# Seven block products instead of eight in more FFN input chunks of a four-layer trunk, and the modulation sums moved to make room

## The reference

```python
def adaln(c, w, b):
    m = (jax.nn.silu(c) @ w + b).reshape(c.shape[0], N_MOD, 1, D_MODEL)
    return [m[:, i] for i in range(N_MOD)]

def swiglu(h, w_in, w_out):
    g, u = jnp.split(h @ w_in, 2, axis=-1)
    return (jax.nn.silu(g) * u) @ w_out
...
for i in range(DEPTH):
    ...
    xp = xp + mod_p[2] * mp
    xs = xs + mod_s[2] * ms
    hp = modulate(rms_norm(xp, norm2_w[i]), mod_p[3], mod_p[4])
    hs = modulate(rms_norm(xs, norm2_w[i]), mod_s[3], mod_s[4])
    xp = xp + mod_p[5] * swiglu(hp, ffn_in_w[i], ffn_out_w[i])
    xs = xs + mod_s[5] * swiglu(hs, ffn_in_w[i], ffn_out_w[i])
```

## Time and profile before

| | us |
|---|---|
| median of 3 runs | 2639.33 |
| lowest and highest | 2639.11, 2639.5 |
| the profiled execution | 2641.69 |
| its span | 2639.7 |
| TensorE busy | 2622.5 |
| VectorE busy | 1814.8 |
| ScalarE busy | 886.7 |
| GpSimd busy | 213.4 |

### The profile page before, as it was taken

One profiled execution on the slowest core, in us unless ns is written; L12 is line 12 of the kernel. 1 busy time (PEld: TensorE's weight loads), 2 busy tenths in 40 slices (PEclk: granted clock), 3 DMA queues, 4 the chain that ended last, 5 costly groups with the idle time before them and its releaser, 6 DMA issues.

```text
span 2639.7 us, 44971 instructions
## 1 busy us (share of the span) xinstructions
PE 2622.5 (99%) x17398; PEld 2551.5 (97%) x17398; DVE 1814.8 (69%) x3097; ACT 886.7 (34%) x1330; POOL 213.4 (8%) x297
## 2 busy tenths in 40 slices
PE   9999999999999999999999999999999999999998
PEld 5999999999999999999967999999999999999998
DVE  5888778676586776846676668768465557748475
ACT  4223331222342222124675432221242234425253
POOL 0000000000000000000000000000000015113020
PEclk9999999999999999999999999999999999999999
DMA  8444445444224454422101245444222224547362
GB/s 308 146 143 138 133 128 176 128 158 143 77 77 128 150 161 124 155 72 74 57 13 73 80 128 160 151 127 152 70 82 72 72 76 112 164 125 187 110 166 76
DMA packets 100025, 321.41 MB, mean 122 GB/s; under 512 B 11712, under 2 KB 14912, under 8 KB 99648
## 3 DMA queue, kind: packets, MB, share of 16 engines
q1 hardware_dynamic: 65776, 211.23, 24.6%
q0 software_dynamic: 34128, 108.54, 14.7%
HBM read 301.12 MB, written 2.88 MB: 115 GB/s over the span
## 4 chain that ended last, share of the span: by engine, by line
PE 94%; DVE 3%; DMA 1%; ACT 1%; issue 1%; DVEq 0%; POOL 0%; SPq 0%; ACTq 0%; POOLq 0%
PE ps L720 40%; PE ps L719 40%; PE ps L772 7%; PE ps_x L1018 1%; PE ps_sum L772 1%; PE ps L994 1%; PE ps L1150 1%; PE ps_sum L1005 1%; DMA mix<-in_ada_head 1%; DVE w_lo L1717 1%; PE ps L1101 0%; PE ps L875 0%; ACT w_hi L1218 0%; PE ps_sum L980 0%; DMA rope<-raw 0%
## 5 line engine op out<-in xcount | busy, mean ns | idle before, releaser
L1717 DVE TENSOR_TENSOR w_lo<-raw,w_hi 128x1024 fp32r<-128x1024 f32 (+2 forms) x319 | 383.1, 1201 | 464.3 <-ACT w_hi L1218 463.1
L1218 ACT ACTIVATE w_hi<-raw 128x1024 fp32r<-128x1024 f32 (+2 forms) x319 | 329.3, 1032 | 917.8 <-PE ps L720 902.8
L719 PE MATMUL ps<-h_hi,w_hi 128*128 128x320 f32 x1568 | 490.6, 313 | 1.3 <-DVE h_lo L2035 0.7
L720 PE MATMUL ps<-h_lo,w_hi 128*128 128x322 f32 x1568 | 489.1, 312 | 0.0
L720 PE MATMUL ps<-h_hi,w_lo 128*128 128x322 f32 x1568 | 488.0, 311 | 0.0
L719 PE MATMUL ps<-h_lo,w_hi 128*128 128x320 f32 x1568 | 487.8, 311 | 0.0
L719 PE MATMUL ps<-h_hi,w_lo 128*128 128x320 f32 x1568 | 487.5, 311 | 0.0
L720 PE MATMUL ps<-h_hi,w_hi 128*128 128x322 f32 x1568 | 486.5, 310 | 0.0
L1745 DVE CUSTOM_DVE_ANT_0 ps_x<-ada_w,cond 128x1024 f32<-128x1024 f32 x354 | 436.0, 1232 | 33.5 <-DVE tmp L1793 13.0
L720 PEld LDWEIGHTS ps<-h_hi,w_hi 128*128 128x128 f32 x1568 | 297.8, 190 | 0.6
L719 PEld LDWEIGHTS ps<-h_hi,w_hi 128*128 128x128 f32 x1568 | 296.0, 189 | 2.4 <-DVE h_lo L2035 0.8
(11 more groups left out here) (239 smaller groups left out, 4014.6 us busy)
## 6 DMA issues: line engine op xcount, KB each, us to landing
raw<-in_weights SPq DMA_DIRECT2D x323, 512.0 KB, 3.6
ada_w<-in_ada_w POOLq DMA_DIRECT2D x177, 512.0 KB, 3.8
raw<-in_weights SPq DMA_DIRECT2D x32, 384.0 KB, 3.0
rope<-in_weights SPq DMA_DIRECT2D x40, 256.0 KB, 3.2
rope<-raw POOLq DMA_DIRECT2D x40, 256.0 KB, 4.1
mix<-in_ada_head SPq DMA_DIRECT2D x16, 512.0 KB, 10.5
raw<-raw POOLq DMA_DIRECT2D x20, 256.0 KB, 3.3
x<-in_x SPq DMA_DIRECT2D x8, 320.0 KB, 10.2
```

Source lines behind the costliest of these rows:

```text
L719: pe.matmul(ps[:, 2 * slot, 0:TA], w[:, slot, ws], a(k)[:, 0:TA], start=begin, stop=end)
L720: mm = pe.matmul(ps[:, 2 * slot + 1, 0:width - TA], w[:, slot, ws], a(k)[:, TA:width], start=begin, stop=end)
L1218: act.activation(w_hi[:, j % 2, 0:tiles * P], raw[:, j, 0:tiles * P] if src is None else src, ACT.Copy).then_inc(w_hi_ready, 1)
L1717: dve.tensor_tensor(w_lo[:, j % 2, 0:tiles * P], raw[:, j, 0:tiles * P] if src is None else src, w_hi[:, j % 2, 0:tiles * P].bitcast(F32), ...
```

## The change

Seven products are used in layer 0 from the second chunk on, in layer 1 in the third, in layer 2 from the first on (again with two plain pairs ahead): `FIRST_SEVEN` becomes `[1, 2, 0, 0]`. In layers 0 and 1 T1 is split in the third quad of the last plain chunk, T2 in the first of its output quads, T3 and T4 at the start of the seven-product chunk; GpSimd makes them between its loads of modulation tiles. `IN_ADA` and `OUT_ADA` now say where sums stand: in seven-product chunks none, but for layer 0's second chunk (one or two per pair, behind the blocks of the first and the second product) and one triple in the plain quad of layers 2 and 3; output quads keep two triples each, except one in layer 2. What no longer fits goes to layer 3's mixer: ten triples with the shares of layer 0's. `kept` makes an output update of layers 2 and 3 wait until its gate has been made. The rotary table is loaded ahead of attention, since `rope` now holds S1 and S2 before it. The loops over the quads of layer 3's mixer are written out.

```diff
-ADA_FFN = [ADA_Q * (n + 1) - (3 if n == 0 else 2) for n in range(DEPTH - 1)]
...
-FIRST_SEVEN = [3, 3, 3, 0]
+FIRST_SEVEN = [1, 2, 0, 0]
+IN_ADA = [[1, [1, 1, 2, 1, 2, 2, 1, 2], 0], [1, 1, 0], [0, 0, 0], [0, 0, 0]]
+OUT_ADA = [[(2, 2), (2, 2)], [(2, 2), (2, 2)], [(2, 2), (2, 1)], [(0, 0), (0, 0)]]
+ADA_CONV = {0: ADA_HEAD, 3: -(-(3 * ADA_T + 2 * KD - ADA_PE) // ADA_N)}
+CONV_TRIPLES = Q_ZU + 2 * Q_B + Q_OUT
+def _in_triples(layer, c):
+    share = IN_ADA[layer][c]
+    if FIRST_SEVEN[layer] == 0 and c == 0:
+        return 1
+    return sum(share) // (2 * ADA_N) if isinstance(share, list) else share * Q_IN
+
+
+def _ada_at(layer, c, out=0):
+
+    if layer == 3:
+        return ADA_CONV[3] + CONV_TRIPLES
+    before = sum(_in_triples(n, i) + sum(OUT_ADA[n][i]) for n in range(layer + 1) for i in range(2) if n < layer or i < c)
+    return ADA_HEAD + CONV_TRIPLES + before + (_in_triples(layer, c) + sum(OUT_ADA[layer][c][:out - 1]) if out else 0)
...
+                        if LAYER_S[layer]:
+                            sp.wait_ge(block_lo_ready, SEVEN * LAYER_S[layer])
+                            sp.wait_ge(s4_made, LAYER_S[layer])
+                        load_consts(((rope, "rope", late_in),))
...
+            def outs_and_first_pair(layer, c, q):
+
+                outs = OUT_ADA[layer][c]
+                for i in range(sum(outs)):
+                    if i == outs[0] + 1:
+                        sums_of_pair(layer, c + 1, 0, q)
+                    ada_triple(_ada_at(layer, c, 1) + i)
...
-                    turn_rows(layer)
+                    for half in range(2):
+                        ada_triple(t + half)
+                        t1_of(layer, 2 * half)
+                        t1_of(layer, 2 * half + 1)
+                    ada_triple(t + 2)
+                    ada_triple(t + 3)
                     for k in range(HALF):
                         t234_of(layer, k)
...
                 def modulation(p, e):
-                    if p // 2 < len(ada):
-                        ada_share(ada[p // 2], 3 * (p % 2) + e, 3 * (p % 2) + e + 1)
+                    share = IN_ADA[layer][c] if isinstance(IN_ADA[layer][c], list) else []
+                    if p < len(share) and e < share[p]:
+                        begin = sum(share[:p]) + e
+                        ada_share(_ada_at(layer, c), begin, begin + 1)
...
+                    if kept:
+                        dve.wait_ge(ada_kept, -(-(ADA_T * layer + KD * GATE2 + m + 1 - ADA_PE) // ADA_N))
...
             def conv(layer, q, g):
-                ada = layer == 0
+                ada = ADA_CONV[layer]
...
                     out_quad(q + half, 4 * half, 2 * layer + 1, gate_of(GATE1), (KD,) * 4, True,
-                             ada=ADA_HEAD + Q_ZU + 2 * Q_B + half if ada else None, turns=layer if half and seven else None)
+                             ada=ada + Q_ZU + 2 * Q_B + half, turns=(layer, 1) if half and seven else None)
...
-                        ffn_in_quad(q, 0, g, pr, r, tiles=(KD, KD, 0, 0), first=(layer, 0, q + 1), turns=layer)
+                        ffn_in_quad(q, 0, g, pr, r, tiles=(KD, KD, 0, 0), first=(layer, 0, q + 1), turns=(layer, 2),
+                                    ada=_ada_at(layer, 0))
```

More of the change, by code:

```diff
@@ L1282, in t2_hi_of, with turn @@
                 act.activation(t2_hi[:, k, :], t2_full[:, k, :], ACT.Identity, scale=-1.0).then_inc(t_hi_ready, 1)
+            def turn(layer, which, j):
+                for k in (T1_ROWS, T2_ROWS)[which - 1][j]:
+                    (t1_hi_of, t2_hi_of)[which - 1](layer, k)
             def t3_hi_of(layer, k):
@@ L1671, in plain_chunk @@
                     count = Q_LAST if edge else Q_IN
-                    with act.Fori(1 if late else 0, count - 1 if edge else count) as i:
+                    turning = c + 1 == FIRST_SEVEN[layer] and not edge
+                    with act.Fori(1 if late else 0, count - (1 if edge else 2 if turning else 0)) as i:
                         ffn_in_quad(i + q, i, 2 * i + r)
+                    if turning:
+                        ffn_in_quad(q + 2, 2, r + 4, turns=(layer, 1))
+                        ffn_in_quad(q + 3, 3, r + 6)
                     if edge:
@@ L1858, in t2_lo_of, with turn @@
                                          op0=ALU.mult, op1=ALU.subtract).then_inc(t_lo_ready, 1)
+            def turn(layer, which, j):
+                for k in (T1_ROWS, T2_ROWS)[which - 1][j]:
+                    (t1_lo_of, t2_lo_of)[which - 1](layer, k)
             def t3_lo_of(layer, k):
@@ L1895, in after_p2 @@
                     refill(p, 2)
[L1896 removed]
+                    modulation(p, 1)
                 def after_p3(p):
@@ L1977, in seven_chunk, with out_quad @@
                 hidden_lo(n - 1)
-            def out_quad(q, m0, n, gate, tiles, squares, folds=True, ada=None, triples=1, first=None, turns=None):
+            def out_quad(q, m0, n, gate, tiles, squares, folds=True, ada=None, triples=1, first=None, turns=None, kept=False):
                 for j in range(4):
@@ L2324, in attention @@
                         shift_lo(2 * layer + 1)
-                    out_quad(q + half, 4 * half, 2 * layer + 1, gate_of(GATE1), (KD,) * 4, True, turns=layer if half and seven else None)
+                    out_quad(q + half, 4 * half, 2 * layer + 1, gate_of(GATE1), (KD,) * 4, True,
+                             turns=(layer, 1) if half and seven else None)
             def tail(q, gate):
@@ L2443, in plain_chunk @@
                         inverse_rms(2 * layer + 1)
-                    with dve.Fori(1 if late else 0, Q_IN) as i:
+                    with dve.Fori(1 if late else 0, Q_IN - 2 if turning else Q_IN) as i:
                         ffn_in(i)
+                    if turning:
+                        ffn_in(2, turns=(layer, 1))
+                        ffn_in(3)
                 for c in range(2):
-                    at = qa + c * (Q_IN + 2 * Q_OUT) if ada else None
                     if c < FIRST_SEVEN[layer]:
-                        plain_chunk(c, at)
+                        plain_chunk(c)
@@ L2458, in _ @@
+                        seven_chunk(layer, 0, q + 1, CHUNK - PLAIN_PAIRS, pr + PLAIN_PAIRS, g + PLAIN_PAIRS, CHUNK)
                     q += Q_IN
-                    out_quad(q, 0, 0, gate_of(GATE2), (KD,) * 4, False, ada=at + Q_IN if ada else None, triples=2)
-                    last_ada = at + Q_IN + 2 if ada else None
-                    if c + 1 < FIRST_SEVEN[layer]:
-                        out_quad(q + 1, 4, 0, gate_of(GATE2), (KD,) * 4, False, ada=last_ada, triples=2)
-                    else:
-                        out_quad(q + 1, 4, 0, gate_of(GATE2), (KD, KD, 0, 0), False, ada=last_ada, triples=2,
-                                 first=(layer, c + 1, q + Q_OUT))
+                    for half, triples in enumerate(OUT_ADA[layer][c]):
+                        ahead = half and c + 1 >= FIRST_SEVEN[layer] and FIRST_SEVEN[layer] < 3
+                        out_quad(q + half, 4 * half, 0, gate_of(GATE2), (KD, KD, 0, 0) if ahead else (KD,) * 4, False,
+                                 ada=_ada_at(layer, c, half + 1) if triples else None, triples=triples,
+                                 first=(layer, c + 1, q + Q_OUT) if ahead else None,
+                                 turns=(layer, 2) if half == 0 and c + 1 == FIRST_SEVEN[layer] < 3 else None,
+                                 kept=c == 0 and FIRST_SEVEN[layer] == 0)
```

160 lines of the change are left out of this document (70 added, 90 removed).

## The result

| | before | after |
|---|---|---|
| median, us | 2639.41 | 2623.32 |
| lowest and highest | 2639.11, 2642.3 | 2619.86, 2624.2 |
| the profiled execution | 2641.69 | 2623.83 |
| its span | 2639.7 | 2621.9 |

The ratio is 0.9935, with a 95% interval from 0.9919 to 0.995. The forecast was 2591 us, its range 2575 to 2610: the sign is right, the size is not, and the time lies outside the range. It is close to the 2626 us that the rival of the port gave; whether for that reason is a question for the experiments.

The account below looks back on a forecast made before the run. TensorE, busy 2622.5 of 2639.7 us, was taken as the bound. 71.3 us of matmuls less 23.4 of losses gives 47.9; from 2641.7 that is 2593.8, and 2.4 lower for the median, 2591 us; range 2575 to 2610.

Parts of the forecast that it names:

- the rival of the port: All layers: GpSimd's additions hold VectorE out for their whole length, 35 us more than forecast, 2626 us; chance 0.07.
- Matmuls removed: 40 newly treated pairs in layers 0 to 2: 480 matmuls fewer at 0.1485 us, 71.3 us less, all on the path.
- Starts of the first seven-product chunk: TensorE waits behind VectorE at each layer's first such chunk: 3.0 us in layer 0, 1.6 in layer 1, 5.5 in layer 2.
- Layer 3's own start: Layer 3's mixer to first FFN quad: added sums make VectorE late, 6 us plus 2.5 for the quad's triple, 8.5 us.
- the rule that it set against this place: Layer 3's second output quad: exclusive port lock, each of six sums behind a GpSimd operation, 5.3 us more, 2597 in all.
- Later chunks of a layer start behind three sums as well, but have no third and fourth combination to wait for: Starts of a layer's later seven-product chunks: no loss, as layer 3's two such starts show no wait.
- Costed at nothing: Turning of rows in layers 0 and 1: covered by VectorE's idle time in the quads; without that cover 3.6 us per layer.
- Transfers, 3.8 us: New seven-product chunks: two cases of TensorE waiting behind an accumulating transfer, 3.8 us; ends 0 and 76 us.
- 1.0 us inside layer 0's second chunk: 12 sums in eight pairs: one per pair fits VectorE's free time, two exceed it; 1 us lost, ends 0 and 17.
- The rival of the transfers: Accumulating transfers collide with raw loads in nearly every pair, 1.9 us each, 2663 us with all 40; chance 0.08.
- the 105 that was named as a sign of failure: Layer 0's second chunk: the forecast is wrong if it takes over 105 us; about 100 to 101 us was expected.
- another such sign: Inside pairs: the forecast is wrong if waits sit there behind accumulating transfers.

Follow-up runs that it names:

- the first kind of hold: The changed kernel, with a pair's raw weight loads inside the chunks, from its third pair on, held until the previous pair's second sum has landed: 2620.92 us, 0.9917.

## Why the prediction was wrong, point by point

- *Matmuls removed, 71.3 us:* right. The count is exact, and the run with short sums and held loads comes within 13 us of the full gain.
- *Starts of the first seven-product chunk:* layer 0 was forecast at 3.0 us and lost 3.15 (2.43 + 0.72); layer 1 at 1.6 and lost 3.76 (2.63 + 1.13); layer 2 at 5.5 and lost 4.05. Together 11.0 against 10.1. That VectorE is behind with sums was right. The place was not: the forecast had TensorE wait at the eighth product, for the third combination, and only the 0.72 and 1.13 us stand there. The 2.43 and 2.63 us stand at the fifth product, for a block's remainder, and layer 2's 3.48 at the fourth, behind ScalarE, which had itself waited 3.75 us for VectorE. The working also had VectorE begin its last update with the chunk; in layer 0 it begins 2.1 us later (443.22 against 441.15). So layer 1's term was less than half of what it cost, layer 2's too large, and that the total fits is in part luck.
- *Layer 3's own start, 8.5 us:* right in sum. Its waits add up to 11.25 us, some 2.5 of which before had; short sums gave 9.6 with the clock. The split was off: 7.4 us more ahead of the first product where 6 was forecast, 1.4 behind it where 2.5 was. Of the six sums of the second output quad four are longer beside GpSimd's additions, by 2.2 us together; the forecast took 3.5, and the rule that it set against this place 5.3.
- *"Later chunks of a layer start behind three sums as well, but have no third and fourth combination to wait for":* **this failed.** 2.60 and 2.45 us were lost there, at layer 0's third and layer 2's second chunk. Layer 3's starts, from which it was argued, have no sums behind their last output units, so they could not show it. VectorE's 5.1 us of update and sums come twice, with 1.44 and 1.80 us of idle for a modulation tile between, and the fifth block's remainder stands behind them; no combination is needed for that. That the new order of GpSimd's loads would make the tiles late is in no term.
- *"Costed at nothing", the turning in layers 0 and 1:* **failed** by 3.4 us, 1.7 in each layer, at the first output quad. The idle time of a whole quad was counted as cover for VectorE's own turning; that GpSimd's additions lengthen the operations beside them, by 4.3 us in the last quad of layer 0's plain chunk, was not counted there, though the prediction had seen it in layer 3.
- *Transfers, 3.8 us, and 1.0 us inside layer 0's second chunk:* **mis-sized.** The waits are 11.3 us in seven places, 1.6 us each, and holding the loads gave 12. The price of one was about right, their number was not: one case in 20 pairs of layer 3 was carried over to the 40 new ones. Five of the seven are in layer 0; why there was not tried apart. The rival of the transfers had this cause at its extreme, and the forecast a third of it. Layer 0's second chunk took 111 us from its first product to its last, over the 105 that was named as a sign of failure, and waits inside pairs behind accumulating transfers, another such sign, came as well. (The new chunks of six pairs took 76 to 83 us, layer 2's of eight 103, where 75 and 100 were forecast.)
- *TensorE's clock:* **missing from the sum.** 14.1 us of busy time, 10 or 11 of it in six windows. Before, no fall of the clock stands behind its waits up to 2560, the longest 1.44 and 1.90 us, so its rows can't show it; that a wait could cost more than its length was not asked.

Without the clock, the waits that were forecast (23.4 us) stand against 39.4: 5.05 at the later starts, 3.4 at the output quads, 6.5 more in transfers, 1 net in the rest. So the waits that were forecast are there in the main, but three things that it put at nothing or did not have (the later starts, the turning beside the sums, the clock) come to some 23 us, 14.1 of it longer busy time, and the collisions were put at less than half of their size.

## What to carry to other kernels

Idle time of a helper engine over a stretch is no cover by itself: ask at each hand-over how far behind that engine is, and put movable work where its lateness can be caught up before the next hand-over, not just ahead of it. Ask the same of the loads that a queue issues in order: a load behind a wait is late for whoever needs it. A wait of some two microseconds on TensorE could cost 1.7 more here, where the clock fell behind it. Where an accumulating transfer is waited for, keep bulk loads off it, up to and past the end of its loop: holding them inside the loop alone only moved the collision to the last turn.

## What was not expected of the hardware

- The clock fell behind single waits of as little as 1.79 us (in the run with the first kind of hold, at 1586), and once behind three of 0.68, 0.81 and 1.22 us within 5 us (at 2137, with all sums short and all loads held), but not behind one of 2.63 us at 1119 in the change. Which waits are followed by a fall, these runs do not settle.
- Matmuls of no use in a wait kept the clock up: 88 more of them, and the median was 5.7 us lower, though within overlapping intervals.
- An operation of VectorE takes longer beside an addition of GpSimd (a sum 1.5 to 2.2 us in place of 1.23), and the addition too (up to 1.97 us at 365 in place of 0.88).
- Executions of one kernel scatter: 2597.4 to 2610.8 us with the sums moved, and only 2593.9 to 2597.3 with the loads held as well.
